# A new order of steps for the RWKV recurrence, with the level sums moved from TensorE and ScalarE to VectorE

## The reference

```
def step(state, inp):
    r_t, w_t, k_t, v_t, kk_t, a_t = inp
    sk = einsum('bhij,bhj->bhi', state, kk_t)
    state = (state * w_t[:, :, None, :]
             - sk[..., None] * (kk_t * a_t)[:, :, None, :]
             + v_t[..., None] * k_t[:, :, None, :])
    y = einsum('bhij,bhj->bhi', state, r_t)
    return state, y
```

## Time and profile before

| what | value |
|---|---|
| median of 3 runs | 2962.39 us |
| time of the profiled execution | 2960.71 us |
| its span | 2958.9 us |
| PE / DVE / ACT / POOL busy, share of the span | 88% / 54% / 33% / 42% |
| mean granted TensorE clock | 0.965 of full |
| recurrence, from the clearing of the state to the next matmul stage | 1621.7 to 2129.9 us |

### The profile page before, as it was taken

How to read it: one execution, slowest core, us unless ns; L and a number is a source line. 1 busy time by engine, 2 the same in 40 slices (tenths; PEclk the granted TensorE clock), 3 DMA queues, 4 the chain that set the end, 5 groups by cost and what they waited for, 6 DMA issues and landing times. The chain is left out here.

```text
span 2958.9 us, 54529 instructions
## 1 busy us (share of the span) xinstructions
PE 2607.3 (88%) x23136; PEld 2118.1 (72%) x23136; DVE 1587.0 (54%) x1909; ACT 966.8 (33%) x1583; POOL 1253.4 (42%) x630
## 2 busy tenths in 40 slices
PE   2787888999999999989898577776699999999999
PEld 1565666888887788767677466666587888788887
DVE  7744545765544534467962766766335443434344
ACT  2434333222223221254443334343334122222221
POOL 3522244444445444354443434353255444444443
PEclk9989999999999999999999799999899999999999
DMA  7511234455532222356576443333232232223233
GB/s 246 186 61 36 86 106 136 135 182 181 182 100 98 90 93 89 100 154 156 140 181 159 107 90 92 86 88 76 82 127 86 88 105 100 86 93 106 94 100 121
DMA packets 299538, 342.15 MB, mean 116 GB/s; under 512 B 215073, under 2 KB 215201, under 8 KB 299297
## 3 DMA queue, kind: packets, MB, share of 16 engines
q1 hardware_dynamic: 299296, 338.66, 38.2%
HBM read 297.77 MB, written 39.85 MB: 114 GB/s over the span
## 5 line engine op out<-in xcount | busy, mean ns | idle before, releaser
L711 POOL TENSOR_TENSOR wl<-w,wh 128x1024 fp32r<-128x1024 f32 x367 | 903.7, 2468 | 1263.9 <-ACT wh L752 1263.7
L181 PE MATMUL ps<-hi,wh 128*128 128x512 f32 x2208 | 881.5, 399 | 26.1 <-ACT qk_raw L789 10.1
L183 PE MATMUL ps<-hi,wl 128*128 128x512 f32 x2208 | 868.0, 393 | 0.0
L182 PE MATMUL ps<-lo,wh 128*128 128x512 f32 x2208 | 867.8, 393 | 0.0
L752 ACT ACTIVATE wh<-w 128x1024 fp32r<-128x1024 f32 x367 | 386.9, 1056 | 690.6 <-DMA w<-in_ffn_w_in 525.6
L181 PEld LDWEIGHTS ps<-hi,wh 128*128 128x128 f32 x2208 | 420.1, 190 | 129.1 <-issue 37.3
L1024 DVE SCALAR_TENSOR_TENSOR xt<-ps,mod,xt 128x512 f32<-128x512 f32 x384 | 286.4, 750 | 415.0 <-PE ps L183 408.8
L182 PEld LDWEIGHTS ps<-lo,wh 128*128 128x128 f32 x2208 | 420.0, 190 | 89.7 <-issue 3.3
L183 PEld LDWEIGHTS ps<-hi,wl 128*128 128x128 f32 x2208 | 418.9, 190 | 89.5
L1029 DVE TENSOR_TENSOR act<-ps,silu 128x512 f32<-128x512 f32 x88 | 60.9, 692 | 461.2 <-PE ps L183 461.2
L181 PE MATMUL ps<-act_hi,wh 128*128 128x512 f32 x704 | 282.7, 402 | 18.0 <-DVE act_lo L1033 10.4
(11 more groups left out here) (227 smaller groups left out, 2978.0 us busy)
## 6 DMA issues: line engine op xcount, KB each, us to landing
w<-in_ffn_w_in SPq DMA_DIRECT2D x176, 512.0 KB, 3.6
piece<-in_ada_w SPq DMA_DIRECT2D x96, 512.0 KB, 4.5
w<-in_ffn_w_out SPq DMA_DIRECT2D x88, 512.0 KB, 3.5
w<-in_w_rkv SPq DMA_DIRECT2D x48, 512.0 KB, 4.0
scratch<-silu SPq DMA_DIRECT2D x48, 256.0 KB, 3.1
scratch<-act SPq DMA_DIRECT2D x48, 256.0 KB, 3.1
w<-in_wqk SPq DMA_DIRECT2D x20, 512.0 KB, 4.8
xt<-in_xT SPq DMA_DIRECT2D x4, 2048.0 KB, 11.4
```

The lines of the kernel that those rows point to most:

```text
L181: pe.matmul(out, w_hi(k), x_hi(k), start=first and k == 0, stop=False)
L182: pe.matmul(out, w_hi(k), x_lo(k), start=False, stop=False)
L183: ins = pe.matmul(out, w_lo(k), x_hi(k), start=False, stop=last and k == kc - 1)
L711: pool.tensor_tensor(wl[n % NW][:, :, :], wr[n % NW][:, :, :], wh[n % NW][:, :, :].bitcast(F32), ALU.subtract).then_inc(*wlo.up)
```

## The change

There are three parts. First, the identity products (L1658) are gone; the product is written to PSUM alone, and VectorE adds the identity while it copies the product out (`level_sum`, an add of PSUM and a constant, three per chunk). ScalarE's three copies `one_plus_x` are gone with it. Second, `level_t` is split into `level_inverse` and `level_transposed` with semaphores of their own, and other helpers are split in the same way (`decays`, `decayed`, `products_b`, `blocks_back`, `finish`), so that their halves can stand apart. Third, the functions `period` of all five engines have a new order, and a seventh stage zq (the gate's product, one chunk later) is added, so that there are 22 periods where there were 21. More waits are written out, since the order no longer implies them. A constant of 64 columns is added to the table of constants that is loaded at the start and used nowhere in what follows.

```diff
+                WITH_IDENT = ()
-                            for j, to, hs in heads():
-                                pe.matmul(spot(0, j, to), idst[hs], idst[hs], start=j % QP == 0, stop=False)
+                            if l in WITH_IDENT:
+                                for j, to, hs in heads():
+                                    pe.matmul(spot(0, j, to), idst[hs], idst[hs], start=j % QP == 0, stop=False)
...
+                        def level_sum(ch, l):
+                            dve.wait_ge(*g["x_done_w"].at(NL * ch + l + 1))
...
+                            dve.tensor_tensor(in_two(wx[l % 2]), two_banks(0), idst.unsqueeze(1).unsqueeze(1).to_broadcast([P, 2, QP, CHUNK]),
+                                              ALU.add).then_inc(*g["w_done"].up)
...
-                        def period(w, x, d, y, zz, zp):
+                        def period(w, x, d, y, zz, zp, zq):
                             if x is not None:
                                 bounded(x)
+                            if y is not None:
+                                level_sum(y, 0)
+                            if x is not None:
+                                decayed_r(x)
                             if d is not None:
-                                invert(d), invert_last(d)
+                                products_k(d), invert(d)
...
-                    for c in range(-RING, NC + 2):
-                        period(at(c + 3), at(c + 2), at(c + 1), at(c), at(c - 1), at(c - 2))
+                    for c in range(-3, NC + 3):
+                        period(at(c + 3), at(c + 2), at(c + 1), at(c), at(c - 1), at(c - 2), at(c - 3))
```

More of the change, by code:

```diff
@@ L76 @@
 C_HALFPI = C_GNEPS + 1
-C_END = C_HALFPI + 1
+C_BLKMASK = C_HALFPI + 1
+C_END = C_BLKMASK + 64
 C_RESET = C_END
@@ L1572, in take_u, with period @@
                             act.activation(in_two(ust), two_banks(3), ACT.Copy).then_inc(*g["ue_done"].up)
-                        def period(w, x, d, y, zz, zp):
+                        def period(w, x, d, y, zz, zp, zq):
+                            if zp is not None:
+                                root(zp)
                             if zz is not None:
-                                take_x(zz)
+                                transposed_out(zz, 2), take_x(zz)
                             if x is not None:
-                                norm_root(x), values_out(x), decays(x), end_decay(x)
+                                end_decay(x), norm_root(x)
                             if y is not None:
-                                level(y, 0)
+                                inverse_out(y, 0)
+                            if x is not None:
+                                values_out(x), decay_before(x)
                             if zz is not None:
@@ L1674, in level_t, with level_transposed @@
+                        def level_transposed(ch, l):
+                            pe.wait_ge(*g["w_done"].at(NL * ch + l + 1))
+                            pe.wait_ge(*g["tt_done"].at(NL * ch + l))
+                            if l == 0:
+                                pe.wait_ge(*tt_in[ch % 2].at(4 * (ch // 2 + 1)))
                             for j, hs, _ in heads():
-                                ins = pe.matmul(bank(2)[hs, j, :], wx[l % 2][hs, j, :], old[hs, j, :], start=True, stop=True)
@@ L1733, in by_feature, with period @@
                             ins.then_inc(*g["yf_done"].up)
-                        def period(w, x, d, y, zz, zp):
+                        def period(w, x, d, y, zz, zp, zq):
+                            if y is not None:
+                                level_x(y, 0)
                             if zz is not None:
-                                known_x(zz)
+                                solve_x(zz)
+                            if d is not None:
+                                gram(d, 1)
+                            if y is not None:
+                                level_inverse(y, 0)
+                            if x is not None:
+                                by_token(x, 0)
                             if zp is not None:
@@ L1767, in period @@
                                 norms(w)
+                            if y is not None:
+                                known_x(y), level_transposed(y, 2)
                         pe.wait_ge(*g["zeros"].at(1))
@@ L1988, in constants @@
     con[:, C_HALFPI] = 0.5 * math.pi
+    con[:, C_BLKMASK:C_BLKMASK + 64] = (np.arange(8)[None, :] > np.arange(8)[:, None]).reshape(1, 64)
     return con
```

304 lines of the change are left out of this document (193 added, 111 removed).

## The result

The changed kernel takes 2908.8 us (median; 2908.74 to 2909.81) against 2961.9 us of the kernel before in the same runs (2953.1 to 2966.95). The ratio is 0.9823, with a 95% interval of 0.9806 to 0.9839. The forecast was 2885 us, with a range of 2852 to 2930: the direction was right and the time lies in the range, but of the 77 us of the sum 53 came. The span of the profiled execution went from 2958.9 to 2907.8 us, 51.1 us less, and 49.3 of them lie in the recurrence: its end, seen as the first load of the phase behind it, moved from 2129.25 to 2079.98 us.

The account below looks back on a forecast made before the run. The prediction took the recurrence's period as a chain of waits, set by VectorE's work plus remaining waits: 22.7 + 1.3 = 24.0 us against 28.67. Gains of 56 + 6 + 15 = 77 us gave 2885.4 us, range 2852 to 2930.

Parts of the forecast that it names:

- the 77 us of the sum: Total gain forecast in the recurrence: 56 us over twelve periods, 6 in the ramp and 15 in the tail.
- The mechanism: VectorE idles 5.9 us per period ahead of the state; the new order fills that place with work TensorE later waits for.
- the signs that were named for the sum: States 23 to 25 us apart, VectorE over 90% busy, under 2 us idle before the state, b_dec and k_dec at 1.5 us or more.
- It gives something only in the tail: Identity products off TensorE: 1.5 to 2.9 us less per period, but TensorE doesn't bound it, so a gain only in the tail.
- Level sums: Three added VectorE instructions per period, priced like masks: 1.88 us more work.
- VectorE's work: 22.7 us per period: 20.4 us now, 1.9 of level sums, 0.4 more of collisions with POOL (3.6 instead of 3.2).
- Waits left: VectorE's remaining waiting per period: 1.3 us of the 8.2 there were, with bounds of 0 and 3.5.
- 22.7 + 1.3 = 24.0: The new period as VectorE's work plus waits left, 24.0 us against 28.67, which gives 56 us over twelve periods.
- Ramp and tail: Gains outside the steady part: 6 us in the ramp (0 to 12) and 15 us in the tail (5 to 22).
- The stops of TensorE: Rival: TensorE's "issue" stops bound the period, not VectorE; period 26.5 us, 39 us gained, 2923 us; chance 0.20.
- Eaten whole: Rival: VectorE stands over 3 us before the inverse for the diagonal's blocks; period 28.5 us, 2955 to 2962 us; chance 0.07.
- The clock: Rival: TensorE's clock stays low for nearly the whole steady part; 16 us slower, 2978 us; chance 0.05.

Follow-up runs that it names:

- e1_swap: The changed kernel with VectorE's inverse of the diagonal moved ahead of the mask ar_k, away from POOL's row of products: 2908.5 us, ratio 0.9831.
- e4_twice_after: The changed kernel with VectorE's mask ar_k done twice per chunk, just ahead of the diagonal's inverse: 2903.7 us, ratio 0.9813.
- e6_twice_late: The changed kernel with VectorE's mask n_t done three times per chunk, between the state and the variance: 2932.7 us, ratio 0.991.
- e7_unalias: The changed kernel with the squares of y in another tile, so that the keys' squares don't wait for the variance: 2892.0 us, ratio 0.9778.
- e12_scan_later: e7_unalias with VectorE's scan of the decays moved behind the bonus, and ScalarE's decay_up with it: 2894.2 us, ratio 0.9784.
- e9_light_loads: The changed kernel with the six operand loads cut to one eighth from the third chunk on: 2902.6 us, ratio 0.9812.
- e10: e9_light_loads with the image transfers of the diagonal blocks also cut to one pair of eight from the third chunk on: 2898.1 us, ratio 0.9793.
- e11: The changed kernel with POOL's second product of the bonus left out: 2898.7 us, ratio 0.9798.

## Why the prediction was right, and where it was wrong

*The mechanism: right.* The order takes the idle time out of the place in front of the state, work fills it, and VectorE is over 90% busy. The order alone is worth 0.9%. Of the signs that were named for the sum, this one and the empty place in front of the state came; the states are 25.9 us apart and not 23 to 25, and `k_dec` takes 0.68 us and not 1.5.

*Operations, by themselves.* "It gives something only in the tail" holds in the old order: 1.0015 for all of them (the sums added to VectorE and the products taken off TensorE could cancel there; they weren't tried apart). In the new order it failed. The identity products are worth about 28 us, over half of the whole gain, because TensorE's level products had become part of the ring. The prediction took 21.0 us busy out of 28.67 as slack; that is an average and says nothing of a wait that closes in every period. Its upper price of a product was also misread: the granted clock from 1719.17 to 1720.12 is 1.00, so the 0.95 us aren't those of the lower level. An identity product there takes 0.84 us (1809.85 to 1810.69, clock 0.53), which makes 1.5 to 2.5 us per period where the prediction has 2.9 at most.

*Level sums.* 1.9 us forecast, 36 instructions of 682 ns, 2.04 us per period with the short overlaps between neighbours counted twice. Right.

*VectorE's work.* 22.7 us forecast, 23.64 measured. The 0.94 us are put down to collisions: 3.6 was taken, some 4.5 came by this difference (5.0 by the means of the groups), over the upper bound of 4.3, and on other instructions than named. I looked for partners among instructions of 512 columns and took the diagonal's inverse as 2.2 us, as it is in the old order. The Trainium skill says in "SBUF — State Buffer" ("SBUF: two separate sides") that such an instruction stands for all of POOL's when POOL's started first. The trace agrees: 165 ns on average before, 1.20 and 1.25 us beside POOL's steps of 1.27. Small ones lose as much as large ones there, and so the most for their size. But the prediction's sum by that rule, 26.8 us of work, was not what came.

*Waits left.* 1.3 us forecast, 2.26 measured, inside the bounds. The places named were partly right: 0.8 us of it is in front of `ar_k`, 0.57 in front of the mean, 0.52 in front of the sums; the diagonal's blocks cost nothing, as forecast.

*The failed step* is the one under both: "22.7 + 1.3 = 24.0". The period is no sum of VectorE's work and a remainder of waits. It is a ring through ScalarE, TensorE, ScalarE, POOL and VectorE, 24.06 us long where TensorE isn't held up and 25.90 on average. The three tests that fix this: taking collisions off VectorE gives nothing (e1_swap), adding 1.3 us gives nothing or costs more than itself by place (e4_twice_after, e6_twice_late), and taking away one wait that is no engine's work gives 1.87 us per period in the profile (e7_unalias). With that wait gone the terms are close to the forecast, 22.94 + 1.09 = 24.03 us, but that is in part luck: in e12_scan_later the work is 0.37 us less and the period 0.31 more. With the sum falls a second sentence of the prediction, that the added waits "are for things that the old order already implied; together nothing, since none stands where an engine is late". The wait at L1547 is one of them. It does stand where an engine is late: ScalarE waits there for 22.4 us in twelve periods. By the profiles this one price at nothing is 12 x 1.87 = 22 us of the 23 that are missing in the steady part (56 against 33); by the ratios it is 13 us.

*Ramp and tail.* 6 us and 15 were forecast, 4.0 and 12.1 came, both inside their bounds. With them 33.2 + 4.0 + 12.1 = 49.3 us in the recurrence, of 77.

*Rivals.* The stops of TensorE didn't become more: 52.1 us in 46 stops over the twelve periods before, 54.0 in 41 after. But the rival's period of 26.5 us is near what was measured, and in part its cause is there too: what lifts the ring from 24.06 to 25.90 us is TensorE's stops and its low clock, which the ring lets through. It is not a bound by itself, since with the ring cut and the full traffic a period is 24.03 us, with 48.8 us of stops. "Eaten whole" needs over 3 us in front of the inverse, which has none.

*The clock.* It didn't stay low (0.93 on average against 0.94). In windows of 1 us it is under 0.75 for 40 us of the twelve periods before, for 40 after and for 14 in e7_unalias. Six of the ten stretches after start right behind a stop on "issue" of 2.2 to 3.2 us, four at or soon behind the norms. So the wait ahead of the norms goes with the fall in some periods only: the clock of the 4 us from their start is 0.50 to 0.62 in four of twelve, and 1.00 in the others, also behind waits of 2.27 and 2.28 us. In e9_light_loads it is under 0.75 in eight of twelve, in e7_unalias in none. How much of e7's gain is the wait and how much the clock wasn't separated. The Trainium skill's page "TensorE: Matmul & The Clock Gate" (Part 1) says that activity lifts the clock. The trace agrees in so far as each of the ten stretches follows a stop or a wait; why other waits have no such stretch behind them, no run here shows. The mean busy share says little, 74% of the steady part after and 73% before.

*Open.* What TensorE does in the stops that come every 250 to 256 records, and whether the last us of the period in e7_unalias is bound by VectorE's work or by the second way through the state products and the mean. The intervals of e9, e10 and e11 against the changed kernel overlap, so their small gains are not shown.

## What to carry to other kernels

Where engines work in fixed orders and hand work around once per period, follow one period through all of them until it closes, and price each change by whether it lies on that ring. Adding the same cheap work at two places of an engine's order finds the ring quickly: here it cost nothing at one place and more than itself at the other. Compare also the shortest interval with the mean one: the first is the ring, and the difference is what it lets through. A wait that a reordering adds for a shared tile has a price like any other: look what stands ahead of it in the new order, not whether the old one implied it.

## What was not expected of the hardware

- A 128x4 product of VectorE with two SBUF inputs took 165 ns on average before and 1.2 us beside a row of POOL's products; four instructions, the first of 128x64, went in step with POOL (starts 1925.85, 1927.14, 1928.43 and 1929.86 against 1925.76, 1927.11, 1928.34 and 1929.69).
- Behind a wait of 1.4 us ahead of the norms the granted clock was 0.50 over the next 4 us, and two sums of squares took 2.08 us instead of 1.12. Behind waits of 2.27 and 2.28 us in other periods it stayed at 1.00.
- TensorE's stops on "issue" come at multiples of 250 to 256 of its records: in 24 of 36 gaps one such number, in ten two to five. The longest was 3.2 us in the changed kernel (2.5 to 3.9 in all with the full traffic) and 1.9 with loads cut to an eighth.
